# Attention with values stationary and scores freed earlier, and the order of the recurrence's cell work changed

## What is computed

```python
# neighbourhood attention: local keys with a bias and a window mask, and 256 context keys
p = jax.nn.softmax(jnp.concatenate([s_loc, s_ctx], axis=-1), axis=-1).astype(v.dtype)
o = einsum('bhjqk,bjkhd->bjqhd', p[..., :n_loc], v_loc) + einsum('bhjqk,bkhd->bjqhd', p[..., n_loc:], v_ctx)

# recurrence (one chunk; six heads, two directions)
a = jnp.cumsum(gc, axis=2)
decay = jnp.exp(jnp.where(causal, a_t - a_s, -inf))
scores = jnp.sum(qc * kc * decay, axis=-1)
o = scores @ vc + (qc * jnp.exp(a)) @ s
s_new = jnp.exp(a_last) * s + (kc * jnp.exp(a_last - a)).T @ vc
```

## Time and profile before

| What | us |
|---|---|
| median of three executions | 4525.09 |
| the profiled execution, its own time | 4534.41 |
| its span in the trace | 4532.6 |
| TensorE busy | 3880.8 (86%) |
| VectorE busy | 2467.1 (54%) |
| ScalarE busy | 1763.4 (39%) |
| granted TensorE clock, mean | 0.895 |

### The profile page before, as it was taken

How to read it: one execution, slowest core, us unless ns; L and a number is a source line. 1 busy time by engine, 2 the same in 40 slices (tenths; PEclk the granted TensorE clock), 3 DMA queues, 4 the chain that set the end, 5 groups by cost and what they waited for, 6 DMA issues and landing times.

```text
span 4532.6 us, 52333 instructions
## 1 busy us (share of the span) xinstructions
PE 3880.8 (86%) x19674; PEld 2996.2 (66%) x19674; DVE 2467.1 (54%) x3567; ACT 1763.4 (39%) x2709; POOL 315.3 (7%) x381
## 2 busy tenths in 40 slices
PE   3996778799896767799999985699997999889998
PEld 2884547566685536455787764578775877567876
DVE  7745662888763493887674315666332332364332
ACT  2124553688422463686322323332232222433222
POOL 2100001100111000000220000021000000000000
PEclk9997658899998857899999997899999999879999
DMA  6531001799463002798574221067322223102222
GB/s 233 192 127 28 1 29 45 269 348 338 160 205 88 1 1 77 270 366 299 189 270 168 93 87 22 27 206 236 131 88 98 96 90 111 71 1 75 93 93 75
DMA packets 185292, 611.65 MB, mean 135 GB/s; under 512 B 39881, under 2 KB 42569, under 8 KB 183913
## 3 DMA queue, kind: packets, MB, share of 16 engines
q1 hardware_dynamic: 117808, 430.60, 27.0%
q0 software_dynamic: 39072, 141.58, 9.4%
q10 hardware_dynamic: 28186, 36.34, 2.7%
HBM read 592.14 MB, written 18.02 MB: 135 GB/s over the span
## 4 chain that ended last, share of the span: by engine, by line
PE 76%; DVE 10%; ACT 6%; issue 3%; DMA 2%; POOL 1%; ACTq 1%; POOLq 0%; DVEq 0%; PEldq 0%; PEld 0%; SPq 0%
PE psum L1908 20%; PE psum L697 10%; PE psum L1921 10%; PE psum L1682 7%; PE psum L755 4%; PE psum L795 4%; PE psum L1701 3%; PE psum L967 2%; PE psum L630 2%; PE psum L954 2%; DVE spare L1036 2%; PE psum L944 1%; POOL spare L532 1%; ACT PB L1005 1%; DVE PB L369 1%
## 5 line engine op out<-in xcount | busy, mean ns | idle before, releaser
L656 DVE TENSOR_TENSOR ring_r<-ring,small_r 128x1024 fp32r<-128x1024 f32 x280 | 343.7, 1231 | 859.0 <-ACT small_r L652 858.7
L652 ACT CAST small_r<-ring 128x1024 fp32r<-128x1024 f32 x280 | 292.1, 1048 | 1210.3 <-PE psum L697 338.5
L652 ACT CAST PB_r<-ring 128x1024 fp32r<-128x1024 f32 x328 | 340.5, 1050 | 543.6 <-PE psum L1908 327.0
L656 DVE TENSOR_TENSOR ring_r<-ring,PB_r 128x1024 fp32r<-128x1024 f32 x328 | 394.4, 1221 | 219.1 <-ACT PB_r L652 218.3
L1908 PE MATMUL psum<-H_r,ring_r 128*128 128x512 f32 x1344 | 335.2, 391 | 0.0
L1908 PE MATMUL psum<-H_r,small_r 128*128 128x512 f32 x1344 | 327.7, 396 | 0.0
L1908 PE MATMUL psum<-H_r,PB_r 128*128 128x512 f32 x1344 | 318.3, 389 | 0.0
L1908 PEld LDWEIGHTS psum<-H_r,small_r 128*128 128x128 f32 x1344 | 253.0, 188 | 60.8
L1908 PEld LDWEIGHTS psum<-H_r,ring_r 128*128 128x128 f32 x1344 | 252.2, 188 | 55.2
L1908 PEld LDWEIGHTS psum<-H_r,PB_r 128*128 128x128 f32 x1344 | 252.3, 188 | 53.2
L697 PE MATMUL psum<-H_r,small_r 128*128 128x512 f32 (+1 forms) x1040 | 272.9, 366 | 5.8 <-issue 5.8
(11 more groups left out here) (377 smaller groups left out, 7272.5 us busy)
## 6 DMA issues: line engine op xcount, KB each, us to landing
ring<-wtile SPq DMA_DIRECT2D x800, 512.0 KB, 4.9
spare<-wmod POOLq DMA_DIRECT2D x97, 512.0 KB, 4.7
H<-wmod POOLq DMA_DIRECT2D x48, 512.0 KB, 3.6
PB<-wmod POOLq DMA_DIRECT2D x48, 512.0 KB, 3.7
X<-wmod POOLq DMA_DIRECT2D x47, 512.0 KB, 5.0
PB<-wmod SPq DMA_DIRECT2D x8, 1024.0 KB, 22.9
X<-x_in ACTq DMA_DIRECT2D x2, 3072.0 KB, 10.9
X<-rpb_rows ACTq DMA_DIRECT2D x24, 224.0 KB, 5.0
```

The lines of the kernel that those rows point to most:

```text
L652: nc.scalar.copy(high(j), slot(g0 + j)).then_inc(high_ready.sem, 1)
L656: nc.vector.tensor_tensor(low(g0 + j), slot(g0 + j), high(j).bitcast(F32), ALU.subtract).then_inc(low_ready.sem, 1)
```

## The change

- In units with heads of 64 channels (both neighbourhood stages and the forgetting one) the product has the values as its stationary side (128x64) and the turned probabilities as its moving side (128 columns). Head 0 writes PSUM partitions 0 to 63 and head 1 partitions 64 to 127, in alternation, so the output is channels by queries. The reciprocals of the sums are spread by two more matmuls (stationary: the reciprocal column broadcast over 64 columns; moving: the identity). ScalarE copies them to SBUF, and VectorE multiplies output by scale straight into the destination. `finish` is gone with its transposes and copies.
- The output has two banks (6 and 7) in all four stages, and VectorE takes it one unit later (u-2). The reciprocal is the first step of VectorE's round.
- A set of score banks is free when its readers are done: `pre` (the new `scores_taken`) and `pre_a`, no longer the maximum.
- `pre_a` of unit u+1 stands ahead of the copies of unit u in ScalarE's list.
- In the recurrence, products for c+1 begin at v=2 (before v=3) and end with `far_product` at v=4 (v=5); exponentials for c+1 begin at v=0 (v=1) and `near_decay` stands at v=1 (v=3) with `magnitude` behind it (at v=0 before); `running` is at v=5 in both layers.

```diff
 def scores(u):
     if u >= NS:
-        eng.wait_ge(scores_read.sem, b_rd + u - NS + 1)
+        eng.wait_ge(scores_taken.sem, b_tk + u - NS + 1)
+        if n_pre[u - NS + 1]:
+            eng.wait_ge(ctx_scaled.sem, b_cs + n_pre[u - NS + 1])
...
 def product(u):
-    if u >= 1:
-        eng.wait_ge(out_copied.sem, b_oc + u)
+    if u >= 2:
+        eng.wait_ge(out_copied.sem, b_oc + u - 1)
...
+    if turned[u]:
         for t in range(nt):
+            for m in range(2):
+                nc.tensor.matmul(ob(u)[64 * m:64 * m + 64, 0:P], units[u]["pv"](m, t), probs(m, t), start=(t == 0), stop=(t == nt - 1))
+        eng.wait_ge(recip_ready.sem, b_rc + u + 1)
+        for m in range(2):
+            mm = nc.tensor.matmul(ob(u)[64 * m:64 * m + 64, P:2 * P], sm(u)[:, m:m + 1].broadcast_to([P, DH]), ident, start=True, stop=True)
...
 # ScalarE
+context_scores(0)
 exponentials(0)
+for u in range(n):
+    context_scores(u + 1)
...
+    exponentials(u + 1)
+    copy_scale(u - 1)
+copy_scale(n - 1)
...
 # VectorE
 maxima(0)
-for u in range(n + 1):
+for u in range(n + 2):
+    if 1 <= u <= n:
+        eng.wait_ge(exp_ready.sem, b_ex + u)
+        nc.vector.reciprocal(sm(u - 1), sm(u - 1)).then_inc(recip_ready.sem, 1)
...
+    if u >= 2:
+        x = u - 2
...
+        if turned[x]:
+            eng.wait_ge(scale_copied.sem, b_sc + n_t[x] + 1)
+            ins = nc.vector.tensor_tensor(units[x]["dst"], ob(x)[:, 0:P], scale(x), ALU.mult)
```

The recurrence, ScalarE and then VectorE:

```diff
-                    if v == 0 and far:
-                        begun = magnitude(c + 2)
-                    if v == 1:
+                    if v == 0 and near:
+                        level_decay(c + 1, 0)
+                        level_decay(c + 1, 1)
+                    if v == 1 and near:
+                        level_decay(c + 1, 2)
+                        near_decay(c + 1)
+                        if far:
+                            begun = magnitude(c + 2)
+                    if v == 2 and near:
+                        far_decay(c + 1)
                         if far:
                             logarithm(c + 2, begun)
...
-                    if v == 2 and far:
+                    if v == 2 and near:
+                        eng.wait_ge(gate_sig.sem, b_gs + c + 2)
+                        level_product(c + 1, 0)
+                        level_product(c + 1, 1)
+                    if v == 3 and near:
+                        level_product(c + 1, 2)
+                        near_product(c + 1)
+                    if v == (3 if l else 4) and far:
                         low_log(c + 2)
...
+                    if v == 4 and near:
+                        far_product(c + 1)
                         if far and l:
                             bounds(c + 2)
...
+                    if v == 5 and far:
+                        running(c + 2)
```

More of the change, by code:

```diff
@@ L907, in rotate, with attention @@
             stage(tensor=ten, vector=vec)
-        def attention(units, S, ET, stats, sc_sets, finish_bank=7):
+        def attention(units, S, ET, stats, sc_sets):
             n = len(units)
@@ L929, in attention @@
             b_ta, b_ca, b_td, b_cd = B(probsT_ready, n_a[n]), B(probsT_copied, n_a[n]), B(hidT_ready, n_d[n]), B(hidT_copied, n_d[n])
-            fins = [u for u in range(n) if units[u]["finish"]]
-            b_fr, b_fc = B(gath_ready, len(fins)), B(gath_copied, len(fins))
+            turned = [units[u]["out"] is None for u in range(n)]
+            n_t = [sum(turned[:u]) for u in range(n + 1)]
+            b_rc, b_sc = B(recip_ready), B(scale_copied, n_t[n])
+            scale = lambda u: small[:, u % 2 * P:(u % 2 + 1) * P]
             mx = lambda u: stats[:, 2 * u:2 * u + 2]
@@ L985, in ten, with context_scores @@
                     scores(u + 2)
-                    finish(u - 2)
                 product(n - 1)
-                finish(n - 2)
-                finish(n - 1)
             def sca(eng):
-                def exponentials(u):
-                    if u >= n:
+                def context_scores(u):
+                    if u >= n or units[u]["pre_a"] is None:
                         return
@@ L999, in exponentials @@
                             eng.wait_ge(hidT_ready.sem, b_td + n_d[u - 1])
-                    if units[u]["pre_a"] is not None:
-                        eng.wait_ge(scores_ready.sem, b_sr + u + 1)
-                        units[u]["pre_a"](eng, Sv(u), sets(u)).then_inc(ctx_scaled.sem, 1)
+                    eng.wait_ge(scores_ready.sem, b_sr + u + 1)
+                    units[u]["pre_a"](eng, Sv(u), sets(u)).then_inc(ctx_scaled.sem, 1)
+                def exponentials(u):
+                    if u >= n:
+                        return
                     eng.wait_ge(max_ready.sem, b_mx + u + 1)
@@ L1032, in maxima @@
                     eng.wait_ge(scores_ready.sem, b_sr + u + 1)
-                    V(eng, units[u]["pre"](eng, Sv(u), sets(u)))
+                    units[u]["pre"](eng, Sv(u), sets(u)).then_inc(scores_taken.sem, 1)
+                    eng.wait_ge(scores_taken.sem, b_tk + u + 1)
                     if units[u]["pre_a"] is not None:
@@ L1115, in neighbourhood @@
                         pre_a=lambda eng, S, bs: nc.scalar.activation(S[:, :, NLAT:NTOK], two_banks(bs[2:], NCTX), ACT.Copy, scale=DH ** -0.5),
[L1116 to L1117 removed]
+                        pv=lambda m, t, pair=pair: VN[:, t, (2 * pair + m) * DH:(2 * pair + m + 1) * DH], out=None, dst=Hv[:, pair, j * P:(j + 1) * P]))
             return units
@@ L1132, in context_attention @@
                         pv=lambda m, t, pair=pair: VN[:, NLAT // P + t, (2 * pair + m) * DH:(2 * pair + m + 1) * DH],
-                        out=scale_rows(OTP[:, j * P:(j + 1) * P]),
-                        finish=([OTP[:, x * P:(x + 1) * P] for x in range(2)], Hv[:, pair, NLAT:NTOK]) if j == 1 else None))
+                        out=None, dst=Hv[:, pair, NLAT + j * P:NLAT + (j + 1) * P]))
             return units
@@ L2043, in differential @@
                     units.append(dict(
-                        nk=nk, width=P, pre=pre, pre_a=None, out=out, finish=None,
+                        nk=nk, width=P, pre=pre, pre_a=None, out=out,
                         qk=[(m, 0, nk, QK2(h)[64 * m:64 * m + 64, j * P:(j + 1) * P], QK2(8 + h)[64 * m:64 * m + 64, 0:nk]) for m in range(2)],
```

106 lines of the change are left out of this document (32 added, 74 removed).

## The result

The kernel before took 4522.56 us (median of four), the changed one 4412.91 us (4402.51 to 4421.87): a ratio of 0.9757, 95% interval 0.972 to 0.9793, so 110 us less. The prediction said 4458, with 4410 to 4500 as range. The sign and most mechanisms were right, and the gain was 1.6 times the one forecast.

A forecast was written before the change was run, and what follows sets the result against it. Neighbourhood stages bound by TensorE or a chain over three engines, recurrences busiest on VectorE. Gains 52 (neighbourhood) + 14 (forgetting) + 3 (differential) - 2 (recurrence) = 67 us, giving 4458 us against the median; range 4410 to 4500.

The forecast's parts named there:

- The round over three engines: Neighbourhood units: closed round from maximum through transposes, copies and context scores; cut, the period falls from 7.20 to 5.3-5.5 us.
- The lower bound of the period: Neighbourhood units: TensorE's list of 5.15 us, one unit's chain of 6.96; the period can't be under 5.46.
- The product: Neighbourhood units: two column halves overlap in pairs, so 24 product instructions take about 1.6 us at full clock.
- the rival that the halves don't overlap: Attention product: column halves don't overlap in long runs, neighbourhood gain 14 us, whole kernel 4507 us; chance 0.07.
- The clock: Forgetting stage: mean clock 0.70, about 0.6 of it at 1.2 GHz; gain per group weighted by that, 1.7 us.
- The clock rival: Attention stages: chip grants 1.2 GHz throughout, TensorE sets the period everywhere, whole kernel 4582 us; chance 0.04.
- Differential: Differential stage: product keeps its form, ScalarE's wait for the maximum stays; gain 3 us, ends 0 and 15.
- Recurrence: Recurrences: cell-boundary waits traded for new VectorE waits at v=3; layer 0 3 us less, layer 1 5 us more.
- The rival of 25 us: Recurrence gains all its boundary waits because ScalarE has slack: 25 us less, whole kernel 4431 us; chance 0.15.
- What follows: Projections, experts and SwiGLU after the changed stages: unchanged and starting earlier, saved time not taken back by a transfer.
- the forgetting stage's term: Forgetting units: eight groups of four at 1.7 us each give 14 us, bounds 4 and 24.
- the neighbourhood's: Neighbourhood stages: 24 units at 1.85 us plus short units and stage ends, 27 and 25, together 52 us.

The follow-up runs named there:

- the lists alone: The kernel before, with score banks freed by their readers and `pre_a` ahead of the copies, product as before: 4469.28 us, 0.9876.
- the values alone: The changed kernel's product, spread scales and two output banks, with banks freed by the maximum, `pre_a` behind the copies, recurrence of before: 4467.97 us, 0.9868.
- the kernel freed by the maximum: The changed kernel, but a score set is free again only after the maximum has run: 4415.97 us, one run.

## Why the prediction was right, and where its sizes were off

- **The round over three engines, right.** The period is 5.15 and 5.41 in turn at full clock, 5.28 in the mean, forecast 5.3 to 5.5, and with `pre_a` behind the copies it is 7.20 again. The prediction named both the freed banks and the place of `pre_a` as the cut; only the place counts. The release a step earlier is worth nothing measurable.
- **The lower bound of the period, wrong by a little.** Both sums behind it came out to the hundredth: TensorE's own list is 5.14 to 5.15 (forecast 5.15), and from a unit's scores to its transposes it is 415.90 - 408.94 = 6.96 (forecast 6.96). The prediction made of the second "one period plus 1.5 us", so that no period could be under 5.46. But what comes on top of the period isn't fixed: it is 1.8 in every second unit. The fixed part is that from the start of the transposes to the next scores, 414.35 - 410.75 = 3.60. So two periods are 6.96 + 3.60 = 10.56 = 419.50 - 408.94.
- **The product, right.** 1.53 for 24 against "about 1.6"; the rival that the halves don't overlap falls by the kernel with the heads in turn. Two of the three changes of form, taken at 0.1 each, show in the weight loads as 0.17 of idle time without a wait, before L973 and before L948; the matmuls themselves stand without a gap there, and since the list adds up to the 5.15 forecast, all three cost no more than the 0.3 forecast. The Trainium skill (TensorEngine Tiling (Array Packing), Key Properties) says that TensorE is drained at such a change; the trace agrees as far as it has a pause in the loads there.
- **The clock: the term that was mis-sized.** I kept the mean clocks of the earlier trace rows for after: in the forgetting stage "0.6 of it at 1.2 GHz", and the neighbourhood units' share with it. After, the clocks are 0.92 to 0.96. So the forgetting stage gave 35 us for 14, and the neighbourhood stages 38 and 31 for 27 and 25. At full clock TensorE isn't the limit of the forgetting stage: it is busy for 81 of 116 us and waits 34 us for the exponentials, while VectorE and ScalarE are as busy as before (93 and 60 us). What the half clock had added on top vanished. That it was the clock is shown for the forgetting stage by the added 384 columns, which raised it and took 21 us off with no other edit. For the neighbourhood stages it is read from the clock rows alone, and what part of the extra 11 and 6 us is the clock's stays open. They lie almost whole in the last stretches: 37.6 to 22.6 us in layer 0, a gain of 15 where the forecast had 5, and 23.0 to 13.2 in layer 1, 10 for 5. Of these stretches 27 and 10 us had run at half clock before and none did after. The middles gave 17.4 and 15.4, what 1.85 per unit makes to within 1 us.
- **The clock rival pointed the wrong way.** It saw less TensorE time and feared that the chip would grant 1.2 GHz throughout. The argument set against it, as many columns in a shorter period, pointed the right way, and I should have carried it into the sum as a gain. That it is the reason isn't shown: in the neighbourhood stages the clock rose with the lists alone, whose product is the old one (0.83 and 0.87 to 0.94 and 0.95), and with the values alone, whose period is still 7.20 (to 0.91 and 0.93). Why only the forgetting stage had been so low stays open too, since the old form ran at 0.83 and 0.87 elsewhere. The Trainium skill (TensorE: Matmul & The Clock Gate, What's actually happening) says that the throttled state is the default and activity releases it; the runs agree where 384 or 512 columns were added, 0.70 to 0.99 and 0.58 to 0.81, and show no effect of 256.
- **Differential, mis-sized.** Forecast 3, with 0 and 15 as ends; it gave 8. The working asked whether the waits for the product go "all" or turn into ScalarE's wait for the maximum, and neither is what came: 13.5 of the 14.9 us went, ScalarE's wait fell by 3, and 8 us came back as VectorE's waits for scores, which the prediction had not looked at. With the 3 us less of busy time that makes 8.
- **Recurrence, right in its mechanism, its sizes partly luck.** The waits came as forecast: in layer 0 those at the boundaries into cells 1 to 4 went from 2.5 to 0.3 or less, and new ones of 1.1 to 1.3 stand at v=3. Layer 1 was 5.0 us longer, the very number forecast, but that depends on the clock of its last stretch: up to there the new order costs 7.6 us, and in two other kernels with it the whole stage took 151.2 and 151.3, no more than before. Layer 0 was 8.9 shorter for 3. With a last stretch as long as before (26.0 against 26.2, the kernel freed by the maximum) it is 5 shorter, 2 of it up to cell 4 and 2.6 between cells 4 and 5; the 3 us that the end of the stage was to give back didn't come, and the other 4 came with the higher clock of the last two cells. Over five kernels of each order the change is worth about 4 us, and I had said 2 slower. The rival of 25 us falls: VectorE's waits for the chunk scores in layer 0 went from 24.1 to 14.6, and in layer 1 from 10.0 to 15.8.
- **What follows, right.** The projections, experts and SwiGLU kept their lengths within 2 us, but for the stretch with the experts behind layer 0, which varies by itself.

In sum: the attention stages gave 112 us (38 + 31 + 8 + 35) where 69 were forecast. Of the 43 between them 21 are the forgetting stage's term, 17 the neighbourhood's and 5 the differential one's.

## What to carry over

Where a stage's mean clock is well under 1, don't price a change to its matmuls at the old mix: work the stage out at full clock too, as a case of its own with a chance, and test it with one useless matmul. When a round over several in-order engines sets the period, look for the one place in one list that closes it before shortening anything; here a product shorter by 1.3 us left the period at 7.20 with that place wrong, and took it from 6.04 to 5.28 with it right. Before you move blocks within ScalarE's list, count what stands ahead of the small copies that others wait for, and spread it. When a stage's length changes from kernel to kernel, cut it at its repeated steps and see which of them move: here all but the last two of seven pieces agreed to 0.1 us.

## What was unexpected of the hardware

- Adding TensorE work made a stage shorter: some 20 us of useless columns, a clock of 0.99 instead of 0.70, and 20.6 us less.
- In the recurrences 256 added columns per chunk left the clock at 0.57 and 0.52, and 512 raised it to 0.81 and 0.71.
- The same recurrence code got a mean clock between 0.50 and 0.58 in kernels that differ only elsewhere, and the stage's length went with it, 163.5 to 155.4 us. All of this lies in its last two cells: the last stretch took 30.1 us with none of it at full clock and 23.9 with 16 us at full clock.
- Matmuls on the two column halves overlap only if they alternate: 0.13 us a pair, against 0.10 for each one when the heads come in turn.
